# Modulation columns of an fp32 two-part network: column layout and a free-axis sum on VectorE in place of column sums on TensorE

## The reference, cut to what matters

```python
cs = jax.nn.silu(c)
for i in range(DEPTH):
    ada = cs @ w_ada[i] + b_ada[i]
    sh1, sc1, g1, sh2, sc2, g2 = [t[:, None, :] for t in jnp.split(ada, 6, axis=-1)]
    u = x * (1.0 + sc1) + sh1
    ...
    x = _layer_norm(DEEPNORM_ALPHA * x + (1.0 + g1) * y, ln_g[i, 0], ln_b[i, 0])
...
c_act = jax.nn.silu(c)
mod = (c_act @ mod_w[i] + mod_b[i])[:, None, :]
kvm = (c_act @ kv_mod_w + kv_mod_b)[:, None, :]
```

## Time and profile before

| | us |
|---|---|
| Median of 3 runs | 3150.53 |
| Lowest and highest | 3142.87, 3151.64 |
| The profiled execution's own time | 3147.85 |
| Its span, from the first to the last instruction | 3146.5 |
| TensorE busy in it | 3004.0 (95%) |
| VectorE busy | 1982.4 (63%) |
| ScalarE busy | 1092.1 (35%) |
| GpSimd busy | 97.6 (3%) |
| Mean granted TensorE clock | 0.985 |

### The profile page before, as it was taken

One profiled execution on the slowest core, in us unless ns is written; L12 is line 12 of the kernel. 1 busy time (PEld: TensorE's weight loads), 2 busy tenths in 40 slices (PEclk: granted clock), 3 DMA queues, 4 the chain that ended last, 5 costly groups with the idle time before them and its releaser, 6 DMA issues.

```text
span 3146.5 us, 46111 instructions
## 1 busy us (share of the span) xinstructions
PE 3004.0 (95%) x19763; PEld 2438.8 (78%) x19788; DVE 1982.4 (63%) x3051; ACT 1092.1 (35%) x1667; POOL 97.6 (3%) x116
## 2 busy tenths in 40 slices
PE   7999999999989999998999898999999998899999
PEld 6876788887866788884868787778887777778887
DVE  6856897787578896877356767554444255554453
ACT  2335432233255432324333333242224344542122
POOL 0000000000000000000002222000000001000000
PEclk9999999999999999998999999999999999999999
DMA  8651554544621545441310000332332220032332
GB/s 258 174 168 59 181 175 159 185 171 156 217 75 36 192 162 180 168 172 43 110 38 13 8 13 10 107 97 94 98 104 82 94 81 27 13 102 94 96 105 81
DMA packets 235520, 346.09 MB, mean 110 GB/s; under 512 B 19620, under 2 KB 119916, under 8 KB 235316
## 3 DMA queue, kind: packets, MB, share of 16 engines
q1 hardware_dynamic: 220740, 331.73, 32.5%
q10 hardware_dynamic: 14576, 11.43, 1.2%
HBM read 340.97 MB, written 2.15 MB: 109 GB/s over the span
## 4 chain that ended last, share of the span: by engine, by line
PE 80%; DVE 13%; ACT 5%; issue 1%; DMA 1%; ACTq 0%; DVEq 0%
PE bank L141 78%; DVE w_tiles L150 2%; DVE w_low L150 2%; PE bank L144 1%; DVE ada_acc L162 1%; ACT w_high L147 1%; DVE x_natural L150 1%; ACT stage L147 1%; DVE w_g L150 1%; ACT w_tiles L147 1%; DVE x_natural L162 1%; ACT L147 0%; DVE x_sm L168 0%; DVE f_a L162 0%; DVE d_sm L168 0%
## 5 line engine op out<-in xcount | busy, mean ns | idle before, releaser
L150 DVE TENSOR_TENSOR w_low<-weight_ring,w_high 128x2048 fp32r<-128x2048 f32 (+2 forms) x212 | 463.8, 2188 | 445.0 <-ACT w_high L147 445.0
L141 PE MATMUL bank<-u_high,w_high 128*128 128x512 f32 x1472 | 578.8, 393 | 14.2 <-ACT u_high L147 6.6
L147 ACT ACTIVATE w_high<-weight_ring 128x2048 fp32r<-128x2048 f32 (+2 forms) x212 | 388.1, 1831 | 581.2 <-DMA weight_ring<-in_mlp_down 178.7
L141 PE MATMUL bank<-u_high,w_low 128*128 128x512 f32 x1472 | 575.3, 391 | 0.0
L141 PE MATMUL bank<-u_low,w_high 128*128 128x512 f32 x1472 | 575.2, 391 | 0.0
L141 PE MATMUL bank<-w_high,u_high 128*128 128x512 f32 x896 | 353.5, 395 | 5.7 <-DVE w_low L150 2.5
L141 PE MATMUL bank<-w_high,u_low 128*128 128x512 f32 x896 | 351.2, 392 | 0.0
L141 PE MATMUL bank<-w_low,u_high 128*128 128x512 f32 x896 | 351.2, 392 | 0.0
L141 PEld LDWEIGHTS bank<-u_high,w_high 128*128 128x128 f32 x1472 | 277.8, 189 | 73.0 <-ACT stage L147 7.6
L141 PEld LDWEIGHTS bank<-u_high,w_low 128*128 128x128 f32 x1472 | 277.8, 189 | 58.6
L141 PEld LDWEIGHTS bank<-u_low,w_high 128*128 128x128 f32 x1472 | 277.9, 189 | 57.2
(11 more groups left out here) (411 smaller groups left out, 4385.5 us busy)
## 6 DMA issues: line engine op xcount, KB each, us to landing
ada_ring<-in_mod_w SPq DMA_DIRECT2D x48, 1024.0 KB, 7.4
weight_ring<-in_f_w_up SPq DMA_DIRECT2D x44, 1024.0 KB, 5.1
ada_ring<-in_w_ada SPq DMA_DIRECT2D x40, 1024.0 KB, 7.1
weight_ring<-in_mlp_up SPq DMA_DIRECT2D x32, 1024.0 KB, 5.4
weight_ring<-in_mlp_down SPq DMA_DIRECT2D x32, 1024.0 KB, 4.9
weight_ring<-in_f_w_down SPq DMA_DIRECT2D x24, 768.0 KB, 4.6
weight_ring<-in_m_w_in SPq DMA_DIRECT2D x16, 1024.0 KB, 9.3
weight_ring<-in_d_w_in SPq DMA_DIRECT2D x12, 1024.0 KB, 5.0
```

The lines of the kernel that those rows point to most:

```text
L141: return self.e.matmul(out, l, r, start=start, stop=stop, skip_group_check=True)
L147: return self.e.activation(out, in_, f, **kw) if self.live else QUIET
L150: return self.e.tensor_tensor(out, a, b, op) if self.live else QUIET
```

## The change

The 48 later blocks are laid out the other way round. The host side hands the three modulation matrices over transposed (`w_ada_cols`, `mod_cols`, `kv_mod_cols`), so that a block's 512 output columns lie on the partitions, four groups of 128, each with its 1024 inputs along the free axis. The silu values are needed as a row on every partition, so ACT stores the two silu vectors to DRAM once (`silu_rows`, 2048 elements of 4 bytes) and loads a row back, broadcast to 128 partitions (512 KB), at six places, into whatever memory is free at the time (`silu_place`). DVE then makes each group's four numbers with one `scalar_tensor_tensor` of 128 by 1024, which multiplies the weights by the row in place and sums along the free axis with its accumulator output (`total`). Four of these and one small addition of the bias make a block. `pe_ada` and `dve_ada_take` are gone, and so are `ada_acc` and its waits.

Some blocks move: `r_out` has none any more, `d_out` has one in each of its two turns, and the last two blocks of the first network's second layer come in `f0_up1`. `squares_junk` moves to where `ada_acc` was. The first four blocks are made as before.

```diff
-        self.aacc = take("ada_acc", [P, 512])
+        self.junk = take("squares_junk", [P, S])
...
-                Linear("d_out", "t", a["d_w_out"][0], 2, wide(0), ada=blocks("m0", 11, 1))]
+                Linear("d_out", "t", a["d_w_out"][0], 2, wide(0), ada=blocks("m0", 11, 1) + blocks("m1", 0, 1))]
...
-        lin += [Linear("r_out", "t", a["rw_wo_2"][0], 2, wide(0), ada=blocks("m1", 11, 1))]
+        lin += [Linear("r_out", "t", a["rw_wo_2"][0], 2, wide(0))]
...
-            src = w[s * 512:(s + 1) * 512, :].rearrange("(k p) n -> p k n", p=P)
-            dst = self.aring[:, s, :].rearrange("p (k n) -> p k n", k=4)
+            src = w[s * 256:(s + 1) * 256, :].rearrange("(j p) k -> p j k", p=P)
+            dst = self.aring[:, s, :].rearrange("p (j k) -> p j k", j=2)
...
-            if i < len(L.ada):
-                self.pe_ada(pe, L.ada[i])
...
+    def act_silu_row(self, a, place, which, key):
+        a.wait_ge(self.silu_out, "rows")
+        a.dma_start(place, self.silu_rows[which].partition_broadcast(P)).then_inc(*self.silu_in.landed(key))
...
+    def dve_ada(self, v, name, i):
+        b = self.lin[name].ada[i]
         _, bias, at, _ = self.ada_blocks[b]
-        v.wait_ge(self.T, "ada", b)
-        v.tensor_tensor(self.mod[:, at:at + 4], self.bank[self.ada_bank.get(b, 7)][:, 0:4], bias, ALU.add).then_inc(
-            *self.V.up("mod", b))
...
+        row, key = self.silu_place(name, i)
+        v.wait_ge(self.silu_in, key)
+        v.wait_ge(self.V)
         for s in range(2):
             v.wait_ge(self.ada_in[s], b)
...
+            for j in range(2):
+                src, total = self.aring[:, s, j * D:(j + 1) * D], self.ada_sum[:, 2 * s + j:2 * s + j + 1]
+                v.scalar_tensor_tensor(src, src, 1.0, row, ALU.mult, ALU.mult, total).then_inc(*self.V.up())
             self.V.mark("ada used", b, s)
-        self.V.mark("ada summed", b)
+        v.wait_ge(self.V)
+        v.tensor_tensor(self.mod[:, at:at + 4], self.ada_sum, bias, ALU.add).then_inc(*self.V.up("mod", b))
...
+        a.wait_ge(self.A, "silu")
+        a.dma_start(self.silu_rows.rearrange("c (j p) -> p (c j)", p=P), self.cs[:], True).then_inc(*self.silu_out.landed("rows"))
...
+        a.wait_ge(self.T, "first", 0)
+        self.act_silu_row(a, self.silu_place("m_qk", 0)[0], 0, "m_qk")
         self.act_m_loads(a)
...
+                if name == "f0_up1" and i == b == 1:
+                    a.wait_ge(self.V, "ada used", L.ada[1], 1)
+                    self.act_silu_row(a, self.silu_top[:], 1, "f0_up1")
...
         self.join(a, self.A, "d heads end")
+        self.act_silu_row(a, self.silu_top[:], 1, "d_out")
         self.act_gate_load(a, "d", self.d_gb[:])
```

More of the change, by code:

```diff
@@ L461, in linears @@
         halves = lambda off: lambda i, q: (i + off) * 256 + q * DFF
-        self.ada_first = blocks("a0", 0, 4)
+        self.ada_first = blocks("first", 0, 4)
         m = a["m_w_in"][0]
@@ L470, in linears @@
                 Linear("f0_dn0", "t", down[0], 2, wide(0), 12, 0, ada=blocks("a1", 8, 2)),
-                Linear("f0_up1", "f", up[0], 5, halves(6), ada=blocks("m0", 0, 5)),
-                Linear("f0_dn1", "t", down[0], 2, wide(0), 10, 12 * P, ada=blocks("a1", 10, 2))]
+                Linear("f0_up1", "f", up[0], 5, halves(6), ada=blocks("a1", 10, 2) + blocks("m0", 0, 3)),
+                Linear("f0_dn1", "t", down[0], 2, wide(0), 10, 12 * P, ada=blocks("m0", 3, 2))]
         d = a["d_w_in"][0]
@@ L493, in linears @@
         at = turn = 0
-        self.ada_bank = {}
         for x in lin:
@@ L760, in pe_linear_t @@
                 self.T.mark("used", w)
-            if i < len(L.ada):
-                self.pe_ada(pe, L.ada[i])
             if between and i == 0:
                 between()
-    def pe_ada(self, pe, b):
-        bank = self.ada_bank.get(b, 7)
-        pe.wait_ge(self.V, "ada summed", b)
-        if bank in self.free:
-            pe.wait_ge(*self.free[bank])
-        for j in range(4):
-            m = pe.matmul(self.bank[bank][:, j:j + 1], self.aacc[:, j * P:(j + 1) * P], self.ones[:, 0:1], True, True)
-        m.then_inc(*self.T.up("ada", b))
-        self.free[bank] = (self.V, "mod", b)
@@ new lines, in silu_place @@
+    def silu_place(self, name, i):
+        if name in ("m_qk", "m_v"):
+            return self.m_o[:, 3, :], "m_qk"
+        if name == "m_o":
+            return self.m_acc[:].rearrange("p a n -> p (a n)"), "m_o"
+        if name in ("d_qk", "d_v"):
+            return self.d_o[:, 3, :], "d_qk"
+        late = name == "f0_dn1" or name == "f0_up1" and i >= 2
+        return self.silu_top[:], "d_out" if name == "d_out" or name[0:2] == "f1" else "f0_up1" if late else "m_out"
+    def dve_ada(self, v, name, i):
+        b = self.lin[name].ada[i]
+        _, bias, at, _ = self.ada_blocks[b]
+        row, key = self.silu_place(name, i)
+        v.wait_ge(self.silu_in, key)
+        v.wait_ge(self.V)
@@ L871, in dve_residual @@
                 xs, tmp = self.X[:, t, i * 512:(i + 1) * 512], self.stage[:, t % 2, :]
-                if t == TT - 1 and i < len(L.ada):
-                    self.dve_ada_take(v, L.ada[i])
                 v.wait_ge(self.T, "sum", name, i, t)
@@ L1107, in pe_first @@
         self.pe_first_turn(pe, 1)
-        self.pe_ada(pe, self.lin["m_qk"].ada[0])
     def pe_first_turn(self, pe, q):
@@ L1264, in act_m @@
         self.act_m_silu(a, 15)
+        a.wait_ge(self.A)
+        self.act_silu_row(a, self.silu_place("m_o", 0)[0], 0, "m_o")
         self.act_gate_store(a, "m")
@@ L1315, in dve_m @@
                 self.dve_ahead(v, "m_qk", 0, 0)
-            self.dve_ada(v, L.ada[i])
+            self.dve_ada(v, "m_qk", i)
             for b in range(4):
@@ L1643, in act_diff @@
     def act_diff(self, a):
+        last = self.lin["f0_dn1"]
+        a.wait_ge(self.T, "used", last.tile(last.turns - 1, len(last.pieces) - 1))
+        self.act_silu_row(a, self.silu_place("d_qk", 0)[0], 1, "d_qk")
         self.act_turn(a, "d u", self.fold[:, 0:8], self.fold[:, 8:16])
```

71 lines of the change are left out of this document (29 added, 42 removed).

## The result

The changed kernel took 3103.42 us in the median of four runs (3091.51 to 3105.19), the kernel before beside it 3148.55 (3142.87 to 3151.64). The ratio is 0.985, its 95% interval 0.982 to 0.988. The prediction was 3103, in a range from 3094 to 3117. Five more runs of the same kernel later gave 3103.47. The profiled execution took 3091.51, the shortest of the nine; its span is 3090.2 us.

The account below looks back on a forecast made before the run. PE was taken as the bound, with DVE close to its limit in f0_up0, f1_up0 and m_qk. Terms 25.4 + 4.7 + 5.5 + 10.7 + 1.6 - 0.4 = 47.5 us gave a 3103 us median, range 3094 to 3117.

Parts of the forecast that it names:

- PE, 0.94 a plain block (25.4): In 27 blocks where only PE bounds the turns on either side, removing the block's matmuls gains 0.94 us each, 25.4 us.
- m_qk, 4.7: In m_qk the wait for bank 0 goes, DVE's splits are late next; 4.7 us gained to the end of turn 3.
- m_o, 5.5: Between m_o's turns the 2.77 us wait, the four matmuls and 1.67 us of slow clock go: 5.5 us.
- f0_up0 and f1_up0, 10.7: DVE's turn with norm rows shortens to 22.4 us, still longer than PE's: 5.2 and 5.5 us gained, 10.7 together.
- Added DMAs: First row lands near 57.7, hidden; store lands by 33; cost to first weight loads up to 2 us, counted as nothing.
- Stage ends and the issue ahead of d_out, 1.2: Ends of stages gain 1.6 us in all; an added DMA issue on ACT ahead of d_out's transposes costs 0.4.
- The sum: Over the whole kernel, all terms together gain 47.5 us, giving a median of 3103 us.
- half rate: Rival in DVE's blocks: accumulating operations need two cycles an element, a block takes 9.5 us; +30 us, 3181; chance 0.11.
- dear read: Rival in DVE's blocks: accumulator read makes an operation 1.5 us; 8 us less gain, 3111; chance 0.22 with late row.
- Given back: Rival in PE's turns: they are paced by the ring, so removing PE work changes nothing, 3150; chance 0.04.

Follow-up runs that it names:

- bare matmuls: Changed kernel (DVE's shorter block kept) with four matmuls of ones put back behind each block's turn, without the old waits: 3129.87 us, 0.994 of the kernel before.
- the run with the waits put back: Changed kernel with four matmuls of ones per block, waiting for DVE's block and the turn's first bank as the old ones did: 3141.03 us, 0.997 of the kernel before.
- PE's part alone: Kernel before without each block's four column-sum matmuls and their waits, DVE's products kept: 3118.05 us, 0.989 of the kernel before.
- the other store: Changed kernel with the silu row stored as 32-byte runs, weight columns permuted to match: 3096.34 us, 0.983 of the kernel before.

## Why the prediction was right, step by step

- **PE, 0.94 a plain block (25.4):** right. Turns without block are 21.77 us apart, with bare matmuls 22.71. From f0_dn0 to the transposes behind f0_dn1, 8 x 0.94 = 7.5 were expected, with 0.2 at the end; it was 7.7 at a clock of 1.00 in both. Block 7 was wrongly among the 27: what follows it waits for DVE's copy, and it gave nothing.
- **m_qk, 4.7:** too high. To the last matmul of turn 3 it was 3.95; the 4.75 at the mark has block 7's 0.81 in it. DVE's block came out 0.5 shorter than I took (4.98 instead of 5.5), and started 1.7 later than I placed it, by the late loads. The first miss made up for a part of the second. The leftover stalls were 0.66 and 0.74 us, under the 1.5 given, with no slow clock behind them.
- **m_o, 5.5:** from the bank that m_v waits for to the cell 7.5 were gained, where my terms for m_v, m_o and the stage's end make 7.8. The wait and the slow clock behind it are gone; in the run with the waits put back the wait alone was 1.37.
- **f0_up0 and f1_up0, 10.7:** too low. f0_up0 gave 6.9 and not 5.2 (at a clock of 0.99 before and 1.00 after, so a part is clock), f1_up0 6.0 and not 5.5, at 1.00 in both. The term that was mis-sized is DVE's turn: 21.96 us and not 22.4, since an accumulating operation takes 1.15 us and not 1.30. So PE waits for no split in those turns at all.
- **Added DMAs:** the step that failed. The store was to land by 33 us, from 11.4 us for half as many elements; it landed at 37.0, behind the first weight loads. I wrote that what it takes from the loads was bounded by 2 us, and counted nothing, "as TensorE starts its first turns on sums, not on loads". The loads were 5 to 8 us late, TensorE's first weight tile among them, and it cost 1.3 to 1.8 us by the end of m_qk: TensorE does start on loads, by way of ACT's and DVE's split of that tile. The first row itself landed at 60.3, 0.6 ahead of the block.
- **Stage ends and the issue ahead of d_out, 1.2:** too small to be told apart in these traces.
- **The sum:** 47.5 expected. In the trace 49.5 up to the r_xn transposes, where 46.6 of mine lie; in the medians 45.1 and 47.5; at equal clock 46.9. Terms that were too high (m_qk, block 7) and too low (f0_up0, f1_up0) partly cancelled, and from d_qk to d_out 7.3 us were gained, some 2 more than my terms there make, at a clock of 0.98 before and 0.99 after. That the median fell on 3103 to half a microsecond is luck: it moves by several with the clock granted.
- **The rivals:** half rate and dear read were refuted in one row, 1.15 us. Their prices were too low, because I took the stages around the cells as having room, which they don't. "Given back" was wrong for the changed kernel. For PE's part alone it was right in the turns with norm rows: there 0.94 a turn came back as a wait for DVE.

## What to carry to other kernels

Where two engines are within a few per cent of each other in a stage, taking work from one alone gives little: in f1_up0 PE's part alone gained 1.7 us, DVE's shorter block alone 2.1, both together 6.0. The change paid because it shortened both. Before moving work to the second engine, compare its turn with the first one's: here DVE's turn with norm rows was already the longer one by 0.2 us, covered by its lead, and a fifth operation in a block made such a turn 1.4 us longer (23.2 for 21.77). And count a store in packets, not in bytes: 8 KB in 2048 pieces made the loads beside and behind it 5 to 8 us late.

## What the runs showed of the hardware

- An accumulating SCALAR_TENSOR_TENSOR with two fp32 sources in SBUF runs as fast as the plain one: 1.22 us for 1024 columns, 1.15 from start to start, and its accumulator read of 0.08 us costs 0.01 (four of them 0.04 in all).
- A store of 2048 elements of 4 bytes took 27.7 us beside weight loads; as 256 runs of 32 bytes 7.0. While the delayed loads were still under way, two issues on ACT took 1.83 us together, against 0.84 in the kernel before and 0.85 with the other store; in the second execution of the changed kernel the loads were as late and the two issues took 0.85, so what lengthens an issue is not shown.
- One stage of the same program took 348 us at a granted clock of 1.00 and 353 at 0.98, in two executions. I had expected less between executions than that.
